# A 128-byte tile declared ahead of the activations: every tile behind it starts 128 bytes later in each partition

## What is computed

```python
def swiglu(h, w_gate, w_up, w_down):
    return (jax.nn.silu(h @ w_gate) * (h @ w_up)) @ w_down
...
h_gate, h_up = jnp.split(xb @ w_gu[e] + b_gu[e], 2, axis=-1)
act = h_gate * jax.nn.sigmoid(SWIGLU_ALPHA * h_gate) * (h_up + 1.0)
return act @ w_down[e] + b_down[e]
```

## Time and profile before

| what | us |
|---|---|
| median of 3 executions | 2050.39 (2049.01 to 2051.85) |
| the profiled execution | 2056.68 |
| its span, first to last instruction | 2054.9 |
| TensorE matmul busy | 1988.8 |
| VectorE busy | 896.2 |
| ScalarE busy | 685.5 |

### The profile page before, as it was taken

How to read it: one execution, slowest core, us unless ns; L and a number is a source line. 1 busy time by engine, 2 the same in 40 slices (tenths; PEclk the granted TensorE clock), 3 DMA queues, 4 the chain that set the end, 5 groups by cost and what they waited for, 6 DMA issues and landing times.

```text
span 2054.9 us, 29208 instructions
## 1 busy us (share of the span) xinstructions
PE 1988.8 (97%) x12315; PEld 1388.9 (68%) x12315; DVE 896.2 (44%) x1076; ACT 685.5 (33%) x944; POOL 54.1 (3%) x42
## 2 busy tenths in 40 slices
PE   8999999999999999999999999999999999999998
PEld 8999778999999887999998444444334333433343
DVE  6766666666666677666644311111111111111112
ACT  5545475445554557544444111111001000100012
POOL 0700000000000000000000002000000000000000
PEclk9999999999999999999999999999999999999999
DMA  9664707555555542555295999999999999999997
GB/s 317 200 212 144 236 1 264 187 184 184 185 185 189 199 152 70 192 194 196 86 329 242 420 427 427 427 428 428 428 429 428 428 428 429 429 429 429 428 427 318
DMA packets 165724, 602.86 MB, mean 293 GB/s; under 512 B 9346, under 2 KB 102486, under 8 KB 140336
## 3 DMA queue, kind: packets, MB, share of 16 engines
q1 hardware_dynamic: 165484, 601.76, 75.3%
q10 hardware_dynamic: 164, 0.04, 0.0%
HBM read 600.68 MB, written 1.09 MB: 293 GB/s over the span
## 4 chain that ended last, share of the span: by engine, by line
PE 72%; DMA 22%; DVE 3%; ACT 2%; issue 0%; SPq 0%; DVEq 0%; ACTq 0%
PE ps L1906 14%; PE ps L1908 14%; PE ps L1907 14%; PE ps L2524 12%; PE ps L2550 5%; DMA sb_raw<-in_moe_w_down 5%; DMA sb_raw<-in_moe_w_gate_up 3%; DMA sb_nat_more<-in_moe_w_gate_up 3%; DMA sb_w_free<-in_moe_w_gate_up 3%; DMA sb_late_raw<-in_moe_w_down 3%; DMA sb_w_free<-in_moe_w_down 3%; PE ps L2489 2%; PE ps L2500 1%; PE ps L2558 1%; ACT sb_w_hi L711 1%; PE ps L2090 1%
## 5 line engine op out<-in xcount | busy, mean ns | idle before, releaser
L1155 DVE TENSOR_TENSOR sb_w_lo<-sb_raw,sb_w_hi 128x2048 fp32r<-128x2048 f32 x175 | 401.9, 2304 | 236.3 <-ACT sb_w_hi L711 235.7
L711 ACT ACTIVATE sb_w_hi<-sb_raw 128x2048 fp32r<-128x2048 f32 x179 | 340.3, 1911 | 169.5 <-PE ps L1908 148.0
L1906 PE MATMUL ps<-sb_xT_hi,sb_w_hi 128*128 128x256 f32 x1344 | 375.1, 279 | 0.0
L1907 PE MATMUL ps<-sb_xT_lo,sb_w_hi 128*128 128x256 f32 x1344 | 374.7, 279 | 0.0
L1908 PE MATMUL ps<-sb_xT_hi,sb_w_lo 128*128 128x256 f32 x1344 | 374.7, 279 | 0.0
L1908 PEld LDWEIGHTS ps<-sb_xT_hi,sb_w_lo 128*128 128x128 f32 x1344 | 255.1, 190 | 0.0
L1907 PEld LDWEIGHTS ps<-sb_xT_lo,sb_w_hi 128*128 128x128 f32 x1344 | 252.5, 188 | 1.5
L1906 PEld LDWEIGHTS ps<-sb_xT_hi,sb_w_hi 128*128 128x128 f32 x1344 | 252.4, 188 | 1.5
L1780 DVE COPY sb_h_rows<-ps 128x512 f32<-128x512 f32 x31 | 21.4, 692 | 314.9 <-PE ps L2524 314.9
L1067 ACT ACTIVATE sb_h_rows<-ps 128x512 f32<-128x512 f32 x32 | 19.1, 598 | 413.3 <-PE ps L2524 413.3
L1907 PE MATMUL ps<-sb_w_lo,sb_a_hi 128*128 128x512 f32 x352 | 138.3, 393 | 0.0
(11 more groups left out here) (333 smaller groups left out, 2698.0 us busy)
## 6 DMA issues: line engine op xcount, KB each, us to landing
sb_raw<-in_moe_w_gate_up SPq DMA_DIRECT2D x49, 2048.0 KB, 34.5
sb_w_free<-in_moe_w_gate_up SPq DMA_DIRECT2D x46, 2048.0 KB, 34.5
sb_raw<-in_ffn_w_up SPq DMA_DIRECT2D x44, 1024.0 KB, 5.3
sb_raw<-in_ffn_w_down SPq DMA_DIRECT2D x44, 1024.0 KB, 5.0
sb_raw<-in_moe_w_down SPq DMA_DIRECT2D x22, 2048.0 KB, 33.9
sb_raw<-in_ffn_w_gate SPq DMA_DIRECT2D x43, 1024.0 KB, 5.4
sb_w_free<-in_moe_w_down SPq DMA_DIRECT2D x21, 2048.0 KB, 33.9
sb_late_raw<-in_moe_w_gate_up SPq DMA_DIRECT2D x17, 2048.0 KB, 35.1
```

The lines of the kernel that those rows point to most:

```text
L711: sc.activation(w_hi[:, c % CUT, :], raw[:, c % RAW, :], ACT.Copy).then_inc(hi_made, 1)
L1155: ve.tensor_tensor(w_lo[:, c % CUT, :], raw[:, c % RAW, :], w_hi[:, c % CUT, :].bitcast(F32), ALU.subtract).then_inc(lo_made, 1)
L1906: pe.matmul(o, l_hi, r_hi, start=start, stop=False)
L1907: pe.matmul(o, l_hi, r_lo, start=False, stop=False)
```

## The change

One tile of 32 fp32 a partition, 128 bytes, is declared ahead of the stack `late`, and lives as long as the kernel. Nothing reads or writes it. No instruction, wait, loop or DMA is added or taken away, and none is moved in order; only the addresses of the tiles behind it grow by 128.

```diff
@@ -163,6 +163,7 @@
         mean_var = sb("mean_var", [P, TB, 2])
 
 
+        sb("shift", [P, 32])
         late = ExitStack()
         narrow_rows = sb("narrow_rows", [P, D], stack=late)
```

## The result

The changed kernel takes 2069.65 us (median of three executions, 2068.85 to 2070.2) where the one before takes 2050.39: a ratio of 1.0088, with a 95% interval of 1.0068 to 1.0107. It is slower by 19.3 us, and lies 10.65 us above the upper end of the predicted range.

What follows compares the result with a forecast made beforehand. TensorE bounds the dense stages to about 1075 us, expert loads on DMA the stretch to about 2035. TensorE, VectorE and ScalarE, and DMA terms of 0 + 0 + 0 left the runs' median, 2050.4 us; range 2041 to 2059.

Steps and rivals of the forecast that it cites:

- the one on TensorE: Dense-stage matmuls: two paces exist at one placement, so a tile's address alone doesn't pick the pace; priced at 0.
- my bounds: Dense feed-forward steps: from 9.0 us less, at the faster pace, to 7.6 us more, or 10.6 at 16.99 us a step.
- 595 and 597 ns: Experts' matmuls with moving rows in `raw` (128 past 512) and `late_raw` (64 past), cited for no effect of address.
- 137 and 137 ns: Experts' weight loads from `xs_even` (64 past) and `h_rows` (32 past), cited for no effect of address.
- Slower steps: Rival: feed-forward steps of phases three and four fall to the pace of one and two, 7.6 us more, 2058.0 us; 17 in 100.
- the count of 18 steps: Steps at 16.40 us, nine each in phases three and four, that could slow to 16.82: 18 x 0.42 = 7.6 us.
- taken to the runs: Whole kernel: zero change to the profiled 2056.7 us, shifted to the runs' median 6.3 us below, 2050.4 us.
- The sign of being wrong: Feed-forward steps: a step taking another time than before in the same phase would mean TensorE's operand addresses matter.
- VectorE and ScalarE at 0: Copies to and from moved tiles cost nothing more; without their idle cover, 1% of VectorE's 709.6 us would be 7 us.
- DMA at 0: Expert loads into the moved slot `late_raw` cost nothing more; even 1% on 24 loads would be 1.2 us.
- That the dense stages' length comes through to the end: Expert loads wait for dense chunks to give up slots, so a microsecond in the dense stages is one at the end.
- The rule of the Trainium skill that the prediction weighed: Loads into `late_raw`: 192 past a 256-byte boundary costs 6 beats against 2 at 64, 4 in 512 dearer.

Runs made afterwards that it cites:

- the opening above: Changed kernel with 384 bytes more ahead of `a`, 2066.99 us; in phase three's opening 71 gate and up matmuls ran at 113.3 ns at distance -64.
- the execution of before that lies near the median: The kernel before, unchanged, profiled a second time: 2051.55 us, span 2049.7, with 31 of the 40 steps at the quicker pace.
- the last kernel: Kernel before with a 128-byte tile ahead of `raw`, two places for `xT` 112 bytes apart, `a` at distance 0 from the weights: 2039.6 us, ratio 0.9946.
- the two kernels with `xT` at 240 past: Kernel before with `xT` 240 past a multiple of 256; `a` kept at -64 in the first (2049.53 us), at distance 0 in the second (2048.35 us).
- both kernels with the head tile: Kernel before with a 128-byte tile ahead of `raw` that moves every tile together (2043.37 us), and the last kernel (2039.6 us).

## Why the prediction was wrong

**The step that failed** is the one on TensorE: "Whatever picks the pace, a tile's address alone doesn't", and from it "I take 0". Two paces at one placement do show that an address alone doesn't pick between them. They don't show that the set to pick from is the same at another address. At +64 the steps of gate and up went at either of two paces; at -64 every step that was traced went at the slower one. A quick pace at -64 isn't ruled out, as the opening above has it; that it doesn't reach the steps there is shown, why it doesn't stays open. For down and the projections the distance sets the pace itself, 229 or 233.3 ns. I had read a state as proof that places don't matter, and left the move of the distance from -64 to +64, which the text names, without a price.

**What took its place**, in terms of the sum: 13.4 us for gate and up, 3.8 for down, 3.8 for the projections, against the execution of before that lies near the median. The last two have no place in my bounds at all: "I bound the price from both sides by the steps" took a step's two lengths as the ends, though a step holds two kinds of matmuls with their operands in opposite roles, and the lengths differ in gate and up alone.

**The rows I leaned on** for the address, "595 and 597 ns" and "137 and 137 ns", are durations of records, and of matmuls with 64 stationary columns whose distances didn't stand beside them. The dense matmuls' price is a spacing from start to start, as in the earlier trace rows; I had not looked at it for the 512-column ones.

**The rival "Slower steps"** (17 in 100, 2058.0 us) had the side and half of the mechanism: phases three and four did fall to 117.8 ns. It was too small for three reasons: 16.91 us and not 16.82 (down), the projections, and the count of 18 steps. That count came from the profiled execution, which was 6.3 us slower than the median and held more of the slower pace than the second one, so that there was more to lose from 2050.4 than from 2056.7: the second one's 31 quick steps give 31 x 0.42 = 13.0 us, nearly the 13.4 that gate and up lost. The sum set against the profiled execution and then "taken to the runs" by subtraction hid this.

**The sign of being wrong** that was named, a step with another time than before in the same phase, doesn't tell the change from chance: phase two of the unchanged kernel has 16.82 us in one execution and 16.40 in the other. The length of 16.91, which neither execution of before has, and the spacing of the 512-column matmuls do tell it.

**What held.** VectorE and ScalarE at 0: 692 and 592 ns as before, and sums of 710.38 and 560.54 us. DMA at 0: loads into `late_raw` at 192 past still have 4.90 us. That the dense stages' length comes through to the end: 13.4 us in the first window, 13.4 in the span.

## What to carry to other kernels

In a stretch that TensorE fills, look at the spacing from one matmul's start to the next for each kind of matmul with the start of its moving and of its stationary tile modulo 256 beside it; a tile that nothing reads can move both of them by 2 to 4%. A pace that differs between stretches of one execution is not evidence that a cause doesn't act: ask which paces remain possible when the cause changes, and take a second trace before its counts become terms of a sum. A change of placement has two customers, matmuls and loads, and they want to be weighed apart.

## What the runs showed of the hardware

**Distance and pace.** On TensorE alone, 512 columns take 226.7 ns at distance 0 and 233.3 at +64, 256 columns settle at 113.3 at -112 and at 116.7 to 121.8 at the others, except for the quicker of the two paces at +64. Matmuls with 64 stationary columns, in the experts, show no such difference between -64 and +64. The Trainium skill, "SBUF — State Buffer", section "Who interferes with whom", gives TensorE one read port for the moving operand and an independent one for weight loads. By that one would expect the distance between the two to make no difference; the runs show up to 3% for 512 columns and 7% for 256. Where in the chip the two reads meet, no run here shows.

**Loads and 256 bytes.** In the last kernel most loads into slots on a multiple of 256 land 4.82 to 4.87 us behind the one before, those into `late_raw`, 128 past, 4.88 to 4.91. A load into `raw` and one into `late_raw`:

```profile
1528.46:1533.28 4.82, 4.78 (x25) 1.81 (x25) 0.69 (x1) 0.60 (x1) 0.00 (x0) 1.00 1.00 428
1538.15:1543.06 4.91, 4.45 (x34) 2.02 (x30) 0.00 (x0) 0.45 (x2) 0.00 (x0) 1.00 1.01 434
```

In the two kernels with `xT` at 240 past it is the other way round: `late_raw` alone lies on a multiple, and has 4.82 to 4.85, the others mostly 4.88 to 4.90. In the second of them, a load into `late_raw` and then one into `nat_more`:

```profile
1505.00:1509.84 4.84, 4.80 (x25) 1.83 (x25) 0.69 (x1) 0.60 (x1) 0.00 (x0) 1.00 1.01 433
1509.84:1514.73 4.89, 4.89 (x28) 2.34 (x30) 2.08 (x3) 1.08 (x2) 0.00 (x0) 1.00 1.00 429
```

A start off the boundary costs about 1%. The rule of the Trainium skill that the prediction weighed ("DMA: Bandwidth & Descriptors", section "How a descriptor splits into AXI transactions") is borne out in that half. The other half, by which 192 past costs more than 64 and which spoke against this change, isn't seen: 64, 128 and 192 past all have 4.88 to 4.91. One slot departs: the middle one of `w_free` mostly keeps 4.89 to 4.90 although it starts on a multiple of 256, in both kernels with the head tile. Why, I don't know.
